# The seam between the expert loop and the second block: residual by identity products, both norms of a tile from one pass

## The chip, the cores and the metric

One core of one Trainium2 chip runs the whole program. The metric is the device time of one execution in microseconds; the kernel before took 2886.91 us (median of three, 2886.65 to 2887.95). The engines are TensorE (PE, and PEld for its weight loads), VectorE (DVE), ScalarE (ACT), GpSimd (POOL) and SyncE (SP), which issues most DMAs. PSUM has eight banks of 128x512 f32, called `bank[0]` to `bank[7]`.

## The reference

Two blocks run one after the other on a sequence of 512 tokens of width 1024. The first ends with an expert layer and a norm; the second starts, in each of its two layers, with a norm of the same `x`:

```
x = x + gt2 * expert_choice_ffn(h, w_router, w_gate, w_up, w_down)
x = rms_norm(x, g_final)                     # end of the first block
h = rmsnorm(x, mix_norm_g[0])                # start of the second block
x = x + mixing_layer(h, ...)                 # x itself is needed again here
```

`rms_norm(x, g)` is `x * rsqrt(mean(x*x) + 1e-6) * g`. The expert layer has 16 experts with 64 tokens each; each expert's result is scaled by its gate and added to the rows of the tokens it took.

## The kernel before

Tokens lie in four tiles of 128 (`TT = 4`); `x` stays on chip as [128, 4, 1024]. Experts run in pairs (`PAIRS = 8`), two experts side by side on 64 rows each. Per pair PE multiplies `xeT` by eight chunks of 1 MB of `w_gate` and eight of `w_up`, turns `hid`, and multiplies `hidT` by eight chunks of `w_down` (`chunk_pair`, line 1804, two chunks at a time). Chunks arrive by DMA in a ring of eight. DVE gates the result into `ye` (L2569), ACT rounds it to `ye_hi` (L721, `split_ye`), DVE takes the rest, `ye_lo` (L2573), and PE scatters both to token rows with `scat_now` in eight pieces of 128x512, `piece = 2 * tile + half` (`scatter`, L1774 and L1775). DVE adds each piece to `x` (`add_scattered`, L2544). For pairs 0 to 6 this is hidden behind the next pair's products; for the last pair it stands alone.

Each engine has its own instruction list, written out by hand and run in order; semaphores (`wait_ge`, `then_inc`) join them. The seam after the last pair goes tile by tile. ACT sums the squares of `x` and takes the root (`tile_rms`, L1004 and L1006), DVE inverts and scales `x` by it and by `g_final` (`moe_scaled`, L2599 and L2601), ACT sums squares of the scaled `x` (`tile_sum`), DVE makes a diagonal matrix of the second norm's factors (`make_diag`, L2577 and L2579), PE turns and scales the tile by it (`turn_tile`, L1889), DVE applies the gain (`take_tile`, L2589, into `h_tmp`), ACT rounds it to `hT_hi` (`tile_hi`) and DVE takes the rest, `hT_lo` (`tile_lo`, L2595). Then PE starts the projections of layer 0 (L1544, L1548, L1549: three products of rounded operands per block). `first_projection` covers the first two tiles, 48 products of 256 columns; it stands behind the turning of all four tiles. What follows waits for all of `hT_lo`.

The weights of the second block come as chunks of 1 MB into `raw[0..3]`. ACT rounds chunk m to `w_hi[m % 2]` (`split(m)`, L721) and POOL takes the rest, `w_lo` (L709). The loads of the first chunks start when PE has used up all but four of the last `w_down` chunks (the POOL engine's wait for `N_LAYER - RING + RAW`); `w_hi[0]` and `w_lo[0]` lie in ring slots of chunks 4 and 5 of the last `w_down`.

## Time and profile before

| | us |
|---|---|
| median of three runs | 2886.91 |
| lowest and highest run | 2886.65, 2887.95 |
| profiled execution | 2892.95 |
| its span | 2891.0 |
| PE busy | 2699.0 (93%) |
| DVE, ACT, POOL busy | 1096.4, 829.0, 697.6 |
| last product of the expert loop starts to run its last chunk | 1631.08 |
| PE goes on without waiting for `hT_lo` | 1671.10 |

The profile is of one execution. Times in the rows are us from the start of the span. A timeline row gives start, duration, engine, line, operation, written and read tiles, how many instructions the row merges, and in brackets how long the engine had been idle and who released it. Busy times of PE are modelled ends of pipelined matmuls, so the distance between starts says more than a duration. PEclk is the granted clock of TensorE: 1.00 is 2.4 GHz and 0.5 is 1.2 GHz.

### The profile page before, as it was taken

To read this page: it belongs to the slowest core of one execution; us is meant where nothing else is said; L and a number is where in the kernel's file an instruction comes from. 1 tells how busy PE (TensorE), PEld (TensorE's weight loads), DVE (VectorE), ACT (ScalarE), POOL (GpSimd) and SP (SyncE) were. 2 spreads that over 40 slices of the span, in tenths; PEclk is the share of its full clock that TensorE was granted. 3 is DMA by queue.
4 is the path that set the end of the run, shared out by engine and by line. 5 is a ranking of instruction groups with operands and counts; after the bars stand their busy time and mean duration, and the time that the engine had idled before them with its cause. 6 is when DMAs were issued, how large, how long until landed. Compare 5 with 4: busy or idle time off the path is not lost.

```text
span 2891.0 us, 35167 instructions
## 1 busy us (share of the span) xinstructions
PE 2699.0 (93%) x14496; PEld 2014.6 (70%) x14496; DVE 1096.4 (38%) x1800; ACT 829.0 (29%) x1444; POOL 697.6 (24%) x297
## 2 busy tenths in 40 slices
PE   7999999999989996999999799999999998999998
PEld 4777777786447885444444397888878896988877
DVE  3555555533341124112121488420014697300034
ACT  2433333333333222000000224532222327322122
POOL 2222222220013410000000032233434332343433
PEclk8999999999999997999999999999999999999999
DMA  7111111102012323899999721123222221223221
GB/s 256 52 58 58 58 58 58 36 30 80 27 39 78 127 92 131 351 409 409 409 408 409 293 84 63 59 73 102 88 96 94 73 88 44 74 89 101 89 100 44
DMA packets 212563, 382.38 MB, mean 132 GB/s; under 512 B 10833, under 2 KB 145877, under 8 KB 211413
## 3 DMA queue, kind: packets, MB, share of 16 engines
q1 hardware_dynamic: 211088, 379.06, 36.4%
q8 instruction: 95, 1.56, 0.2%
q10 hardware_dynamic: 1349, 1.51, 0.2%
q14 instruction: 31, 0.25, 0.0%
HBM read 378.44 MB, written 2.10 MB: 132 GB/s over the span
## 4 chain that ended last, share of the span: by engine, by line
PE 69%; DMA 8%; issue 7%; DVE 5%; PEld 5%; ACT 3%; POOL 2%; DVEq 1%; PEldq 0%; SPq 0%; ACTq 0%; POOLq 0%
PE bank L1544 14%; PE bank L1548 13%; PE bank L1549 13%; PE bank L1804 7%; DMA ring<-in_w_up 4%; DMA ring<-in_w_gate 3%; PE bank L1749 2%; PE bank L1692 2%; PEld bank L1352 2%; PE bank L1412 1%; PE bank L1421 1%; PE bank L1598 1%; PE bank L1425 1%; PE bank L1615 1%; PE bank L1318 1%
## 5 line engine op out<-in xcount | busy, mean ns | idle before, releaser
L709 POOL TENSOR_TENSOR w_lo<-ring,w_hi 128x2048 fp32r<-128x2048 f32 x96 | 446.3, 4649 | 1279.0 <-ACT w_hi L721 1279.0
L721 ACT ACTIVATE w_hi<-ring 128x2048 fp32r<-128x2048 f32 (+1 forms) x114 | 215.0, 1886 | 676.4 <-PE bank L1544 676.3
L1544 PE MATMUL bank<-hT_hi,w_hi 128*128 128x512 f32 (+1 forms) x928 | 357.1, 385 | 9.2 <-DVE hT_lo L2595 7.7
L1548 PE MATMUL bank<-hT_lo,w_hi 128*128 128x512 f32 (+1 forms) x928 | 352.8, 380 | 0.0
L1549 PE MATMUL bank<-hT_hi,w_lo 128*128 128x512 f32 (+1 forms) x928 | 349.4, 377 | 0.0
L1804 PE MATMUL bank<-ring,xeT 128*64 128x512 f32 x992 | 225.5, 596 | 30.8 <-DMA ring<-in_w_gate 18.5
L1544 PEld LDWEIGHTS bank<-hT_hi,w_hi 128*128 128x128 f32 x928 | 175.8, 189 | 45.7 <-DVE hT_lo L2595 8.5
L2786 DVE TENSOR_TENSOR ffn_hT<-ffn_sg,bank 128x512 f32<-128x512 f32 x44 | 30.3, 688 | 449.1 <-PE bank L1549 449.1
L1549 PEld LDWEIGHTS bank<-hT_hi,w_lo 128*128 128x128 f32 x928 | 175.5, 189 | 35.7
L1548 PEld LDWEIGHTS bank<-hT_lo,w_hi 128*128 128x128 f32 x928 | 174.9, 189 | 31.8 <-issue 1.0
L1804 PEld LDWEIGHTS bank<-ring,xeT 128*64 128x64 f32 x992 | 77.0, 137 | 155.5 <-issue 152.9
L1318 PE MATMUL bank<-hT,head_w 128*128 128x512 f32 x336 | 157.0, 593 | 0.0
L678 POOL TENSOR_TENSOR w_lo<-ring,w_hi 128x2048 fp32r<-128x2048 f32 x16 | 73.6, 4602 | 331.5 <-ACT w_hi L721 331.5
L2780 DVE TENSOR_TENSOR ffn_lo<-ffn_hT,ffn_hi 128x1024 fp32r<-128x1024 f32 x22 | 98.1, 4457 | 118.6 <-ACT ffn_hi L721 118.6
L1544 PE MATMUL bank<-w_hi,ffn_hi 128*128 128x512 f32 x352 | 138.1, 392 | 4.0 <-DVE ffn_lo L2780 4.0
L1548 PE MATMUL bank<-w_lo,ffn_hi 128*128 128x512 f32 x352 | 137.7, 391 | 0.0
L1549 PE MATMUL bank<-w_hi,ffn_lo 128*128 128x512 f32 x352 | 137.6, 391 | 0.0
L1804 PE MATMUL bank<-ring,hidT 128*64 128x512 f32 x512 | 112.3, 594 | 3.8 <-DMA ring<-in_w_down 2.9
L1544 PE MATMUL bank<-w_hi,hT_hi 128*128 128x256 f32 x384 | 109.2, 284 | 5.0 <-POOL w_lo L709 3.3
L2645 DVE SCALAR_TENSOR_TENSOR conf<-glu,cols_l,conf 128x512 f32<-128x512 f32 x120 | 111.3, 957 | 6.6 <-issue 1.3
L655 POOL TENSOR_TENSOR intra<-decay,tri 128x512 f32<-128x512 f32 x16 | 20.3, 1266 | 384.5 <-ACT decay L844 384.5
L1549 PE MATMUL bank<-w_hi,hT_lo 128*128 128x256 f32 x384 | 108.3, 282 | 0.0
(492 smaller groups left out, 5058.2 us busy)
## 6 DMA issues: line engine op xcount, KB each, us to landing
ring<-in_w_gate SPq DMA_DIRECT2D x86, 1024.0 KB, 9.1
ring<-in_w_down SPq DMA_DIRECT2D x86, 1024.0 KB, 14.1
ring<-in_w_up SPq DMA_DIRECT2D x82, 1024.0 KB, 14.1
ring<-in_w_in SPq DMA_DIRECT2D x33, 1024.0 KB, 5.2
head_w<-in_w_in SPq DMA_DIRECT2D x32, 512.0 KB, 5.3
mod_w<-in_w_mod SPq DMA_DIRECT2D x8, 2048.0 KB, 8.5
ring<-in_w_out SPq DMA_DIRECT2D x12, 1024.0 KB, 4.8
ring<-in_w_mod SPq DMA_DIRECT2D x8, 1024.0 KB, 16.4
```

Of the source, the lines that this page charges most:

```text
L678: pool.tensor_tensor(w_lo[m % 2][:], raw[merge_raw(m)[0]][:], w_hi[m % 2][:].bitcast(F32), ALU.subtract).then_inc(lo_ready, 1)
L709: pool.tensor_tensor(w_lo[m % 2][:], raw[m % RAW][:], w_hi[m % 2][:].bitcast(F32), ALU.subtract).then_inc(lo_ready, 1)
L721: return act.activation(dst, src, ACT.Copy)
L1318: last = mm(bank[0 if s == 1 else 1][:], head_w[:, k, s * HD:(s + 1) * HD], hT[:, k, :], start=k == 0, stop=k == KD - 1)
L1352: last = mm(bank[2][:, t * P:(t + 1) * P], hT[:, k, t * P:(t + 1) * P], head_w[:, k, 3 * HD:4 * HD], start=k == 0, stop=k == KD - 1)
L1544: first = mm(dst, a[0], b[0], start=start, stop=False)
L1548: mm(dst, a[0], b[1], start=False, stop=False)
L1549: return mm(dst, a[1], b[0], start=False, stop=stop)
L1692: last = mm(bank[t % 2 * 2 + c // 2][:, c % 2 * 256:(c % 2 + 1) * 256], mT[:, k, t * P:(t + 1) * P], kview(N_OUT + c)[:, k, :], start=k == ...
L1804: last = mm(bank[banks + hf][a * 64:a * 64 + 64, :], lhs[:, 2 * j + kk, a * 64:a * 64 + 64], chunk[a][:, kk, hf * 512:(hf + 1) * 512], sta ...
L2645: stt(conf[:, b, :], glu[:, b, j:j + SEQ], w, conf[:, b, :], ALU.mult, ALU.add)
L2780: tt(ffn_lo[:, j % 2], ffn_hT[:, 2 * j:2 * j + 2, :], ffn_hi[:, j % 2].bitcast(F32), ALU.subtract)\
```

## The change

PE: after the last pair's transposes, `keep` copies `x` into banks by products with the identity (four products of 128x512 before the down projection, two after its first chunk pair, two after its end), and the last pair's scatter accumulates on them, piece n in bank n. `scatter` no longer waits for DVE's adds. `turn_tile` uses banks 2t and 2t+1 for the first norm.

DVE: in place of adding a piece to `x`, `moe_gained` multiplies the bank by `g_final` into `x`. `moe_eps` makes the term that takes the place of epsilon, from the sum of squares of the unscaled tile. The norm's factor itself (`rstd[:, 4:8]`) is computed once for the four tiles at the end.

ACT: a table load for the root stands behind the last pair's last copy, `split(0)` stands ahead of `split_ye` (it waits for the sixth of the eight last `w_down` chunks to be used up), `moe_sums` sums the squares of both banks of a tile and of the gained tile, and takes one root. The copies `ident_r` and `causal_r` move behind the last tile. `x` is multiplied by the factors of the first norm in four activations between the second sigmoid and `split(3)` of layer 0.

The diff:

```diff
--- before.py
+++ after.py
@@ -1059,17 +1059,17 @@
                 copy(hidT[:, 0:4, :].rearrange("p k n -> p (k n)"), bank[0][:]).then_inc(sem("hidT_act"), 1)
                 if pair + 1 < PAIRS:
                     gathered(pair + 1)
-            split_ye(PAIRS - 1)
-
-
-            reached(act, "block2_consts")
-            copy(ident_r[:], ident[:])
-            copy(causal_r[:], causal[:]).then_inc(step["mask_parts"], 1)
+            LAST = (PAIRS - 1) * 8
+            act.activation(rms[:, 0:1], eps_col[:, 0:1], ACT.Sqrt)
 
             def split(m):
 
                 act.wait_ge(raw_landed[m % RAW], 16 * (6, 6, 2, 2)[m % RAW] + 16 * (l * PER_LAYER // RAW + m // RAW + 1))
-                parts_free(act, m, l)
+                if l + m == 0:
+
+                    act.wait_ge(chunk_used, N_LAYER - 2)
+                else:
+                    parts_free(act, m, l)
                 copy(w_hi[m % 2][:], raw[m % RAW][:]).then_inc(hi_ready, 1)
 
             def tile_sum(n, t):
@@ -1095,21 +1095,39 @@
                 parts_free(act, M_DOWN + j, l)
                 copy(ffn_hi[:, j % 2], ffn_hT[:, 2 * j:2 * j + 2, :]).then_inc(sem("ffn_hi_ready"), 1)
 
+            def moe_sums(t):
+
+                act.wait_ge(sem("scattered"), LAST + 2 * t + 2)
+                act.drain()
+                for hf in (1, 0):
+                    if hf == 0:
+                        act.wait_ge(sem("x_added"), LAST + 2 * t + 1)
+                    act.activation(sq_junk[:, hf * 512:(hf + 1) * 512], bank[2 * t + hf][:], ACT.Square,
+                                   accum_out=ss[:, 4 * hf + t:4 * hf + t + 1]).then_inc(sem("moe_rms"), 1)
+                act.wait_ge(sem("x_added"), LAST + 2 * t + 2)
+                act.drain()
+                act.activation(sq_junk[:], x[:, t, :], ACT.Square, accum_out=ss[:, 8 + t:9 + t])
+                act.wait_ge(sem("x_tile"), TT + t + 1)
+                act.drain()
+                act.activation(rms[:, t:t + 1], ss[:, 8 + t:9 + t], ACT.Sqrt, scale=1.0 / DM, bias=pinv2[:, t, 1:2])\
+                    .then_inc(sem("rms_ready"), 1)
+
             l = 0
             split(0)
-            act.activation(sq_junk[:, 0:1], eps_col[:, 0:1], ACT.Sqrt)
-            for t in range(TT):
-                act.wait_ge(sem("x_added"), (PAIRS - 1) * 8 + 2 * t + 2)
-                act.drain()
-                tile_rms(4 + t, t, "moe_rms")
-                if t:
-                    tile_sum(0, t - 1)
-                if t >= 2:
-                    tile_hi(0, t - 2)
-            tile_sum(0, TT - 1)
-            tile_hi(0, TT - 2)
+            split_ye(PAIRS - 1)
+            moe_sums(0)
+            moe_sums(1)
+            tile_hi(0, 0)
+            moe_sums(2)
+            tile_hi(0, 1)
+            moe_sums(3)
+            tile_hi(0, 2)
             split(1)
-            tile_hi(0, TT - 1)
+            tile_hi(0, 3)
+            act.activation(rms[:, 4:8], pinv2[:, 0:TT, 0], ACT.Sqrt, scale=1.0 / DM).then_inc(sem("moe_rms"), 1)
+            reached(act, "block2_consts")
+            copy(ident_r[:], ident[:])
+            copy(causal_r[:], causal[:]).then_inc(step["mask_parts"], 1)
             for l in range(LAYERS):
                 cols_l, lam_i = cols_ls[l], lam_is[l]
                 for b in range(2):
@@ -1118,6 +1136,11 @@
                         .then_inc(sem("glu_sig"), 1)
                     if b == 0:
                         split(2)
+                if l == 0:
+                    act.wait_ge(sem("x_added"), PAIRS * 8 + 1)
+                    act.wait_ge(sem("turned"), 3 * KD)
+                    for t in range(TT):
+                        act.activation(x[:, t, :], x[:, t, :], ACT.Copy, scale=rstd[:, 4 + t:5 + t])
                 for m in range(3, 7):
                     split(m)
 
@@ -1763,7 +1786,15 @@
                     last = mm(bank[4][:, 0:EXPERTS], onehot[:, t, pair * P:(pair + 1) * P], aff[:, t, :], start=t == 0, stop=t == TT - 1)
                 last.then_inc(sem("slots_done"), 1)
 
-            def scatter(pair, piece, dst):
+            def keep(pieces):
+
+                for piece in pieces:
+                    t, hf = piece // 2, piece % 2
+                    if piece >= 6:
+                        pe.wait_ge(sem("ye_gated"), 2 * PAIRS - 2 + hf + 1)
+                    mm(bank[piece][:], ident[:], x[:, t, hf * 512:(hf + 1) * 512], start=True, stop=False)
+
+            def scatter(pair, piece, dst, start=True):
 
                 t, hf = piece // 2, piece % 2
                 if piece == 0:
@@ -1771,7 +1802,7 @@
                 if piece < 2:
                     pe.wait_ge(sem("ye_ready"), pair * 2 + hf + 1)
                 rows, cols = scat_now[:, t * P:(t + 1) * P], slice(hf * 512, (hf + 1) * 512)
-                mm(dst, rows, ye_hi[:, cols], start=True, stop=False)
+                mm(dst, rows, ye_hi[:, cols], start=start, stop=False)
                 mm(dst, rows, ye_lo[:, cols], start=False, stop=True).then_inc(sem("scattered"), 1)
 
             def scatter_behind(pair, pieces):
@@ -1829,16 +1860,20 @@
                         last.then_inc(sem("hid_turned"), 1)
                 if pair + 1 < PAIRS:
                     gather(pair + 1, 1)
+                else:
+                    pe.wait_ge(sem("scat_ready"), PAIRS)
+                    keep((2, 3, 4, 5))
                 pe.wait_ge(sem("hidT_act"), pair + 1)
                 pe.wait_ge(sem("hidT_dve"), pair + 1)
                 for j in range(4):
                     chunk_pair(2, hidT, 6, j)
+                    if pair + 1 == PAIRS and j == 0:
+                        keep((0, 1))
             pe.drain()
             pe.sem_inc(parts_used, 2)
+            keep((6, 7))
             for piece in range(8):
-                if piece >= 4:
-                    pe.wait_ge(sem("x_added"), (PAIRS - 1) * 8 + piece - 3)
-                scatter(PAIRS - 1, piece, bank[piece % 4][:])
+                scatter(PAIRS - 1, piece, bank[piece][:], start=False)
 
 
             reached(pe, "block2_consts")
@@ -1882,8 +1917,8 @@
             def turn_tile(n, t, free_parts=False):
 
                 pe.wait_ge(sem("diag_ready"), n * TT + t + 1)
-                b0 = 2 * t if n and n % 2 == 0 else 2 * (t % 2) + (0 if n else 4)
-                if t >= 2 and (n % 2 or not n):
+                b0 = 2 * (t % 2) if n % 2 else 2 * t
+                if t >= 2 and n % 2:
                     pe.wait_ge(sem("h_ready"), n * KD + 2 * (t - 2) + 2)
                 for k in range(KD):
                     last = mm(bank[b0 + k // 4][:, k % 4 * P:(k % 4 + 1) * P], x[:, t, k * P:(k + 1) * P], diag[:, t, :],
@@ -2581,7 +2616,7 @@
             def take_tile(n, t):
 
                 dve.drain()
-                b0 = 2 * t if n and n % 2 == 0 else 2 * (t % 2) + (0 if n else 4)
+                b0 = 2 * (t % 2) if n % 2 else 2 * t
                 gains = cols_ls[n // 2][:, L_FFN if n % 2 else L_MIX:]
                 for hf in range(2):
                     dve.wait_ge(sem("turned"), (n + 2) * KD + 2 * t + hf + 1)
@@ -2594,32 +2629,44 @@
                     ks, ts_ = slice(4 * hf, 4 * hf + 4), slice(t * P, (t + 1) * P)
                     tt(hT_lo[:, ks, ts_], h_tmp[:, hf], hT_hi[:, ks, ts_].bitcast(F32), ALU.subtract).then_inc(sem("hT_lo_ready"), 1)
 
-            def moe_scaled(t):
-                dve.wait_ge(sem("moe_rms"), t + 1)
-                dve.reciprocal(rstd[:, 4 + t:5 + t], rms[:, 4 + t:5 + t])
-                dve.drain()
-                stt(x[:, t, :], x[:, t, :], rstd[:, 4 + t:5 + t], gfin_b[:], ALU.mult, ALU.mult)
-                dve.drain().then_inc(sem("x_tile"), 1)
+            def moe_gained(t):
+                for hf in range(2):
+                    c = slice(hf * 512, hf * 512 + 512)
+                    dve.wait_ge(sem("scattered"), (PAIRS - 1) * 8 + 2 * t + hf + 1)
+                    if hf:
+                        dve.wait_ge(sem("moe_rms"), 2 * t + 1)
+                    tt(x[:, t, c], bank[2 * t + hf][:], gfin_b[:, c], ALU.mult).then_inc(sem("x_added"), 1)
+
+            def moe_eps(t):
+
+                dve.wait_ge(sem("moe_rms"), 2 * t + 2)
+                ts(pinv2[:, t, 0:1], ss[:, t:t + 1], ss[:, 4 + t:5 + t], DM * EPS, ALU.add, ALU.add)
+                dve.drain()
+                ts(pinv2[:, t, 1:2], pinv2[:, t, 0:1], EPS / DM, None, ALU.mult).then_inc(sem("x_tile"), 1)
 
             dve.wait_ge(sem("row_b_in"), 64)
-            for t in range(TT):
-                for piece in (2 * t, 2 * t + 1):
-                    add_scattered(PAIRS - 1, piece, bank[piece % 4][:])
-                if t:
-                    moe_scaled(t - 1)
-                if t >= 2:
-                    make_diag(0, t - 2)
-                if t == 3:
-                    take_tile(0, 0)
-                    tile_lo(0, 0)
-            moe_scaled(3)
+            moe_gained(0)
+            moe_eps(0)
+            moe_gained(1)
+            make_diag(0, 0)
+            moe_eps(1)
+            take_tile(0, 0)
+            make_diag(0, 1)
+            moe_gained(2)
+            tile_lo(0, 0)
+            moe_eps(2)
+            take_tile(0, 1)
             make_diag(0, 2)
-            take_tile(0, 1)
+            moe_gained(3)
             tile_lo(0, 1)
+            moe_eps(3)
+            take_tile(0, 2)
             make_diag(0, 3)
-            for t in (2, 3):
-                take_tile(0, t)
-                tile_lo(0, t)
+            tile_lo(0, 2)
+            take_tile(0, 3)
+            tile_lo(0, 3)
+            dve.wait_ge(sem("moe_rms"), 2 * TT + 1)
+            dve.reciprocal(rstd[:, 4:8], rms[:, 4:8]).then_inc(sem("x_added"), 1)
             reached(dve, "block2_consts")
             dve.drain()
             rope_buf = rope_2
```

On ACT, from the last `hidT` copy of the expert loop to the roots of the first two tiles. Before (`sq_junk,ss<-x` is the sum of squares of a tile, `rms` its root, `w_hi_210<-ring_52` is `split(0)`):

```order
L721 ACTIVATE hidT<-bank 128x512
L721 ACTIVATE ye_hi<-ye 128x512 x2
L721 ACTIVATE ident_r<-ident 128x128
L721 ACTIVATE causal_r<-causal 128x128
L721 ACTIVATE w_hi_210<-ring_52 128x2048
L1100 ACT_TABLE_LOAD
L1100 ACTIVATE sq_junk<-eps_col 128x1
L1004 ACTIVATE sq_junk,ss<-x 128x1024
L1006 ACTIVATE rms<-ss,eps_col 128x1
L1004 ACTIVATE sq_junk,ss<-x 128x1024
L1006 ACTIVATE rms<-ss,eps_col 128x1
L1004 ACTIVATE sq_junk,ss<-x 128x1024
```

After:

```order
L721 ACTIVATE hidT<-bank 128x512
L1063 ACT_TABLE_LOAD
L1063 ACTIVATE rms<-eps_col 128x1
L721 ACTIVATE w_hi_210<-ring_52 128x2048
L721 ACTIVATE ye_hi<-ye 128x512 x2
L1105 ACTIVATE sq_junk,ss<-bank 128x512 x2
L1109 ACTIVATE sq_junk,ss<-x 128x1024
L1112 ACTIVATE rms<-ss,pinv_227 128x1
L1105 ACTIVATE sq_junk,ss<-bank 128x512 x2
L1109 ACTIVATE sq_junk,ss<-x 128x1024
L1112 ACTIVATE rms<-ss,pinv_227 128x1
```

`split(0)` and the table load now stand ahead of the two `ye_hi`, and one root per tile stands where two stood, behind two sums from banks and one from `x`.

On DVE, from the last `ye` to the first rounded rest. Before (`x<-x,bank` adds two pieces of a tile, `x<-x,rstd,gfin_b` scales it):

```order
L2569 SCALAR_TENSOR_TENSOR ye<-bank,gate_col,gt_b 128x512 x2
L2573 TENSOR_TENSOR ye_lo<-ye,ye_hi 128x512 x2
L2544 TENSOR_TENSOR x<-x,bank 128x512 x4
L2599 RECIPROCAL rstd<-rms 128x1
L2601 SCALAR_TENSOR_TENSOR x<-x,rstd,gfin_b 128x1024
L2544 TENSOR_TENSOR x<-x,bank 128x512 x2
L2599 RECIPROCAL rstd<-rms 128x1
L2601 SCALAR_TENSOR_TENSOR x<-x,rstd,gfin_b 128x1024
L2577 RECIPROCAL rstd<-rms 128x1
L2579 TENSOR_SCALAR diag<-ident,rstd 128x128
```

After (`x<-bank,gfin_b` is the gained tile, `pinv_227` holds the epsilon term):

```order
L2604 SCALAR_TENSOR_TENSOR ye<-bank,gate_col,gt_b 128x512 x2
L2608 TENSOR_TENSOR ye_lo<-ye,ye_hi 128x512 x2
L2638 TENSOR_TENSOR x<-bank,gfin_b 128x512 x2
L2643 TENSOR_SCALAR pinv_227<-ss 128x1
L2645 TENSOR_SCALAR pinv_227<-pinv_227 128x1
L2638 TENSOR_TENSOR x<-bank,gfin_b 128x512 x2
L2612 RECIPROCAL rstd<-rms 128x1
L2614 TENSOR_SCALAR diag<-ident,rstd 128x128
L2643 TENSOR_SCALAR pinv_227<-ss 128x1
L2645 TENSOR_SCALAR pinv_227<-pinv_227 128x1
L2624 TENSOR_TENSOR h_tmp<-bank,cols_l 128x512 x2
L2612 RECIPROCAL rstd<-rms 128x1
```

The scaling by the first norm and its reciprocal are gone from between the tiles, and the first `h_tmp` stands before the third tile's pieces.

## Rows read from the trace of the kernel before

**Rows 1.** The page's busy times: engine, us, share of span, instructions.

```profile
PE 2699.0 (93%) x14496; PEld 2014.6 (70%) x14496; DVE 1096.4 (38%) x1800; ACT 829.0 (29%) x1444; POOL 697.6 (24%) x297
```

**Rows 2.** Stages: length; busy PE, PEld, DVE, ACT, POOL; PEclk, DMA share, GB/s.

```profile
1641.15:1648.40 7.25, 0.00 (x0) 0.02 (x1) 5.75 (x9) 5.73 (x13) 2.55 (x1) 0.66 0.48 157
1648.40:1654.80 6.40, 6.35 (x32) 6.17 (x32) 5.45 (x10) 3.25 (x7) 0.00 (x0) 0.58 0.47 150
1654.80:1663.20 8.40, 5.30 (x31) 5.12 (x32) 6.56 (x13) 5.20 (x12) 0.00 (x0) 0.80 0.01 2
```

**Rows 3.** Timeline of PE, last pair's transposes to first scatter.

```profile
1615.06 1.25 PE L1827 MATMUL bank<-ident,hid 128*128 128x128 f32 x8 [0.79 <-DVE hid L2561]
1617.14 7.38 PE L1804 MATMUL bank<-ring,hidT 128*64 128x512 f32 x32 [0.83 <-ACT hidT L721]
1625.96 3.65 PE L1804 MATMUL bank<-ring,hidT 128*64 128x512 f32 x16 [1.45 <-DMA ring<-in_w_down]
1631.08 3.65 PE L1804 MATMUL bank<-ring,hidT 128*64 128x512 f32 x16 [1.47 <-DMA ring<-in_w_down]
1637.07 0.47 PE L1774 MATMUL bank<-ye_hi,scat_now 128*128 128x512 f32 x1 [2.33 <-DVE ye_lo L2573]
```

**Rows 4.** Timeline of DVE in the seam.

```profile
1637.87 2.48 DVE L2544 TENSOR_TENSOR x<-x,bank 128x512 f32<-128x512 f32 x4 [0.29 <-PE bank L1775]
...
1642.43 2.35 DVE L2601 SCALAR_TENSOR_TENSOR x<-x,rstd,gfin_b 128x1024 f32<-128x1024 f32 x1
...
1646.33 1.28 DVE L2601 SCALAR_TENSOR_TENSOR x<-x,rstd,gfin_b 128x1024 f32<-128x1024 f32 x1
...
1658.85 1.29 DVE L2595 TENSOR_TENSOR hT_lo<-h_tmp,hT_hi 128x512 fp32r<-128x512 f32 x2
```

**Rows 5.** Timeline of ACT in the seam.

```profile
1637.16 1.90 ACT L721 ACTIVATE w_hi<-ring 128x2048 fp32r<-128x2048 f32 x1
...
1640.64 1.06 ACT L1004 ACTIVATE sq_junk<-x 128x1024 f32<-128x1024 f32 x1
...
1641.86 0.30 ACT L1006 ACTIVATE rms<-ss,eps_col 128x1 f32<-128x1 f32 x1
...
1662.19 1.23 ACT L721 ACTIVATE hT_hi<-h_tmp 128x512 fp32r<-128x512 f32 x2 [1.38 <-DVE h_tmp L2589]
```

**Rows 6.** Timelines of POOL, DVE and PE: weight rests, last `hT_lo`, its waiter.

```profile
1639.14 4.56 POOL L709 TENSOR_TENSOR w_lo<-ring,w_hi 128x2048 fp32r<-128x2048 f32 x1 [517.77 <-ACT w_hi L721]
...
1665.31 4.58 POOL L709 TENSOR_TENSOR w_lo<-ring,w_hi 128x2048 fp32r<-128x2048 f32 x1 [21.61 <-ACT w_hi L721]
...
1665.78 4.66 DVE L2595 TENSOR_TENSOR hT_lo<-h_tmp,hT_hi 128x512 fp32r<-128x512 f32 x1 [0.25 <-ACT hT_hi L721]
...
1671.10 0.38 PE L1544 MATMUL bank<-hT_hi,w_hi 128*128 128x256 f32 x1 [1.95 <-DVE hT_lo L2595]
```

**Rows 7.** Timelines elsewhere: f32 products, a turned tile, a 512-wide activation with accumulator.

```profile
517.30 4.03 PE L1318 MATMUL bank<-hT,head_w 128*128 128x512 f32 x9
...
1661.43 2.05 PE L1889 MATMUL bank<-diag,x 128*128 128x128 f32 x16 [0.47 <-DVE diag L2579]
...
1776.06 0.72 ACT L1144 ACTIVATE p<-bank,nmax 128x512 f32<-128x512 f32 x1
```

**Rows 8.** Line 573 from 1620 to 1660: the first five raw loads.

```profile
L573 SPq DMA_DIRECT2D ring<-in_w_in x5: 367/583/3912, 1624.6 to 1644.1; - x5
...
DMA to landing us min/median/max: 5.3/9.4/12.7
```

**Rows 9.** ACT in layer 0: timeline; last row by line (busy us, mean ns).

```profile
1688.15 0.69 ACT L1117 ACTIVATE sig<-bank,cols_l 128x512 f32<-128x512 f32 x1 [3.34 <-PE bank L1549]
1690.23 1.92 ACT L721 ACTIVATE w_hi<-ring 128x2048 fp32r<-128x2048 f32 x1 [1.39 <-PE bank L1544]
1701.65 1.92 ACT L721 ACTIVATE w_hi<-ring 128x2048 fp32r<-128x2048 f32 x1 [9.51 <-PE bank L1544]
...
L727 ACT ACTIVATE xn<-x 128x1024 f32<-128x1024 f32 x4 | 4.2, 1041 | 0.0
```

## The prediction

> **What bounds the kernel now.** Read first the busy shares: TensorE (PE) is busy 93% of the span [rows 1], so only a stretch where PE idles can give time back without removing PE work. The change touches one such stretch, the seam between the expert loop and layer 0 of the second block. The stages [rows 2] show it: PE is busy 0 of 7.25 us, then 6.35 of 6.40 (at a mean granted clock of 0.58, so mostly at 1.2 GHz), then 5.30 of 8.40. Before the seam PE waits for DMA: in the last down projection it stands idle 1.45 and 1.47 us for `in_w_down`, and 0.83 us for `hidT` [rows 3]. After it PE works without holes from 1671.10, when it stops waiting for the last `hT_lo` [rows 6]. So the time that counts runs from 1634.73, the end of the last expert product (1631.08 + 3.65, [rows 3]), to 1671.10: **36.4 us**. I judge the change by when this second point comes. Up to the last pair's down projection both kernels issue the same work.
>
> In between four engines hand one tile on to the next. VectorE (DVE) makes `ye` and `ye_lo`, PE scatters, DVE adds, ScalarE (ACT) sums squares for the first norm, DVE scales `x`, ACT sums for the second norm, DVE makes `diag`, PE turns the tile, DVE and ACT split it. Then `split(1)` on ACT (1.90 us as `split(0)`, [rows 5]) wakes GpSimd (POOL), and the last `hT_lo` is caught behind POOL's 4.58 us [rows 6].
>
> **Part 1, the identity products.** `keep` puts `x` into the eight banks by eight products of 128x512 in f32. The nearest row is the f32 product of the same shape, 9 records in 4.03 us [rows 7], or 0.45 us each. An f32 product is two records: one turned tile is 8 products in the program and 16 records in 2.05 us [rows 7]. So one identity product costs 0.90 us and six of them, placed before the end of the down projection, cost 5.4. Idle time to hide in is 0.83 + 1.45 + 1.47 = 3.75 [rows 3]. Step by step: the transposes are through at 1616.2, `keep(2..5)` runs to 1619.8, chunks 0 and 1 of w_down (3.65 each) surround `keep(0,1)` and end at 1628.9 in place of 1624.5, chunk 2 ends at 1632.5 and chunk 3 at **1636.2, not 1634.73: +1.5 us**. Bounds: 0 if a product is one record (2.7 us for six, all hidden), 1.7 if all of 5.4 − 3.75 shows. I take 1.5.
>
> The Trainium skill ("FP8 and Floating Point Precision", TensorE Precision Notes) says that true FP32 takes four passes, and "TensorE: Matmul & The Clock Gate" (Wait — 56ns, not 53.3ns?) gives 215.7 ns for 512 columns; by these one product is 0.86 us (an estimate) and this part costs 0.2 us less.
>
> **Part 2, the first weight split moved ahead of `split_ye`.** `split(0)` needs `raw[0]`. Its load is issued when chunk 1 of w_down is used up, at 1624.60 before, and landed 9.4 us later, at 1634.0, because it queues behind w_down; an undisturbed one takes 5.3 [rows 8]. Now it is issued at 1629.0 and lands at about 1634.3. ACT then splits for 1.90 us [rows 5], to 1636.25, and is free when `ye_gated` comes at 1637.0, so ACT itself delays nobody. But POOL starts `w_lo` 0.08 us after a split ends and holds on for 4.56 us [rows 6]: 1636.3 to 1640.9. The next thing that DVE must do is `ye_lo` from `ye` and `ye_hi`, ready at 1637.7. What happens to a DVE operation with two SBUF inputs under POOL's `w_lo` is in the rows: the `x` scaling took 2.35 us where the others took 1.28 [rows 4] and ended 1.08 after POOL; `hT_lo` took 4.66 where two take 1.29 [rows 4, 6] and ended 0.55 after POOL. Adds from a bank, with one SBUF input, kept their pace, four in 2.48 us, although POOL was on for half of that [rows 4, 6]. So `ye_lo` waits until 1640.9 + 0.55 = 1641.45, and the first scatter starts at **1641.5 in place of 1637.07 [rows 3]: +4.4 us**. This swallows the 1.5 us of part 1, since `raw[0]`, not PE, sets the time. Bounds: 1.8 without the hold (PE finishes `keep(6,7)` at 1638.8), 4.9 if `raw[0]` lands 0.5 later. I take 4.4. The Trainium skill ("SBUF — State Buffer", Who interferes with whom) says that whichever of the two starts first keeps the shared ports for its whole instruction. The rule speaks against this place for the split, and the rows bear it out.
>
> The other side: the same `w_lo` no longer holds up the first `x` scaling (1.07 us), and `split(0)` and the load of a function table behind it no longer stand between `ye_hi` and the first norm on ACT, which started at 1640.64 though its tile was complete by 1639.2 (1637.87 and two adds, [rows 4, 5]). Both gains lie inside the next part.
>
> **Part 3, both norms at once.** Removed per tile: one reciprocal and the 1.28 us scaling on DVE, and the round trip ACT, DVE, ACT between the two norms. Added: two Squares of 512 from banks on ACT, the two small `pinv2` operations on DVE. Prices: a 512-wide activation from a bank with accumulator took 0.72 [rows 7] (I use 0.76 for the one behind a drain and 0.68 for the next); Square of 1024 with its read 1.22 (from start to start, [rows 5]) and the root 0.33; DVE 0.65 for a bank operation (2.48 / 4, [rows 4]) and 0.42 for the `pinv2` pair (two small ones of about 0.2, priced like a reciprocal); a turned tile 1.95 at 2.4 GHz. I wrote out both orders engine by engine, each instruction starting 0.04 us after the later of its engine and its releaser. For the kernel before, with its own slow clock stretches, this gives 1671.1 against 1671.10, so the bookkeeping holds.
>
> For the kernel after, from the first scatter at 1641.5: two pieces 1.2, tile 0's sums and root 3.2, tile 1's 3.1 (1649.0), waiting for tile 0 turned and split 2.2, tile 2 5.2, tile 3 5.2, so `hT_hi` of tile 2 is done at 1661.6. Before, that point was 1663.42 (1662.19 + 1.23, [rows 5]), or 26.35 us after the first scatter; now 20.1. **−6.3 us.** Behind it nothing is new: split 1.9, POOL 4.6, `hT_lo` 1.3, which gives 1669.4. The 48 products of the first projection (5.6 us) start at 1663.5 and end at 1669.1, just as late: no more can be won here without both.
>
> Sum: +4.4 − 6.3 + 0.2 (rounding over the tail) = **−1.7 us** at full clock.
>
> **Part 4, what moves behind the seam.** ACT scales `x` in four activations of 1.04 [rows 9], 4.2 us between the second sigmoid and `split(3)`. That split started at 1690.23, the next one waited for PE until 1701.65 [rows 9]. 4.2 us after the sigmoid's end at 1688.8 means start 1693.0, then 1.9 + 4.9 on POOL: ready at 1699.9, needed at 1701.6. Hidden, with 1.7 us left; if that cover goes, it costs what exceeds it. DVE's long convolution loses its POOL overlap a little differently; I add 0.2. And the clock: with the scatter at +4.4 PE idles some 2.7 us, and tiles are turned in short bursts 5 us apart, so a slow stretch over one burst is likely. The mean of 0.80 over 8.40 us before the first projection [rows 2] means 3.4 us at 1.2 GHz; laid over one tile after another such a piece costs the chain 0 to 1.4; I add 0.5. **Net −1.0 us.**
>
> **Rivals.** (A) **No hold**: DVE gets through, or `w_lo` comes too late to meet `ye_lo`. Against it stand the two held operations of rows 4 and 6, for it only a DVE that is ready before POOL is. The scatter starts at 1638.8, the chain is then bound by the first projection and ends at 1666.5: −4.6, 2882.3; with cheap products as well −6.2, 2880.7. (B) **The clock stays at 1.2 GHz** from the hold through the turned tiles and into the first projection. For it: in the stretch before, it stayed low through tile turning that kept PE busy 6.35 of 6.40 us [rows 2]. Through the turns only, it costs 3.5 and gives +1.8, 2888.7. If it stays low through the 48 products too, they take 11.2 us: +9.0, 2895.9. It decides from the moment PE enters the first projection, at 0.5 us lost per us: to be slower by 5.8 us takes 8 of those 11 us at 1.2 GHz. (C) **The cost falls on layer 0**: `split(3)` slips past its 1.7 us and PE waits: −1.0 + 1 to 4, 2887 to 2890. (D) The removed round trip wins less, since Squares from banks take 1.1 us, not 0.7: +2.0, 2887.9.
>
> **How the numbers follow.** The profiled execution took 2892.95 (span 2891.0 and 1.95 around it), 6.0 above the median of 2886.91; a shift of 1 us is carried over to the median as it is. Forecast 2886.91 − 1.0 = **2885.9**. A measurement of this kernel can tell 0.2%, 5.8 us, from no change. Chances: forecast within 2 us 0.52; A 0.16, of which 0.04 beyond −5.8; B 0.12, of which 0.06 beyond +5.8; C and D 0.11; something that I don't see 0.09, of which 0.06 faster and 0.02 slower. So faster 0.10, same 0.82, slower 0.08. The range reaches to A and to the mild end of B and C: 2881.8 to 2890.5.
>
> **What would show it.** Right: `keep` records of about 0.45 us pitch and the last expert product ending 1.5 us later; POOL's `w_lo` starting before `ye_lo`, and `ye_lo` at 3.5 to 4.5 us; the first scatter 4.4 later; the tail from first scatter to `hT_hi` of tile 2 at 20 us; no new PE wait for `w_lo` behind `split(3)`. Wrong: `ye_lo` at 0.7 us, a PE wait for POOL near 1700, or a granted clock of 0.5 inside the first projection.

## The result, and the profile after

| | before | after |
|---|---|---|
| median of 15 runs each, us | 2888.74 | 2892.73 |
| lowest and highest, us | 2885.19, 2893.35 | 2889.35, 2898.01 |
| profiled execution, its span, us | 2892.95, 2891.0 | 2892.73, 2890.9 |
| PE, DVE, ACT, POOL busy, us | 2699.0, 1096.4, 829.0, 697.6 | 2703.8, 1099.2, 833.2, 697.1 |

The changed kernel is **slower by 4 us**: the ratio is 1.0014, interval [1.0007, 1.002]. The forecast was 1 us faster, 2885.9, worked out from a median of three runs (2886.91); fifteen runs of the kernel before give 2888.74. The result is less than the 5.8 us that the prediction took as the least that can be told, but its interval lies wholly above 1. Forecast and result are both small against the runs' own scatter of 8 us, and the two profiled executions differ by 0.1 us in span. That the spans agree is chance: from 2278.41 to 2299.50, far behind the change, the trace of before has a stretch at a mean granted clock of 0.66 (2285 to 2290), and the same distance between two `w_lo` is 21.09 us there and 19.58 after. So the place is read from distances inside each trace, not from the spans.

The page's busy times of the kernel after [answers rows 1] show PE up by 4.8 us (the identity products are 7.6, and less of the seam ran at the slow clock: the mean granted clock from 1640 to 1680 is 0.91 instead of 0.83) and ACT up by 4.2, about the scaling of `x` (the norms' own work on ACT is 12.3 us before and 12.6 after):

```profile
PE 2703.8 (94%) x14512; PEld 2012.7 (70%) x14512; DVE 1099.2 (38%) x1801; ACT 833.2 (29%) x1453; POOL 697.1 (24%) x297
```

**The seam on PE**, timeline of after [rows 3]: start, duration, operation, number merged, idle time before and its releaser.

```profile
1614.59 1.25 PE L1858 MATMUL bank<-ident,hid 128*128 128x128 f32 x8 [0.79 <-DVE hid L2596]
1615.68 3.60 PE L1795 MATMUL bank<-x,ident 128*128 128x512 f32 x8
...
1624.71 10.52 PE L1835 MATMUL bank<-ring,hidT 128*64 128x512 f32 x48
1636.11 1.98 PE L1795 MATMUL bank<-x,ident 128*128 128x512 f32 x4 [0.88 <-DVE ye L2604]
1641.18 0.47 PE L1805 MATMUL bank<-ye_hi,scat_now 128*128 128x512 f32 x1 [3.09 <-DVE ye_lo L2608]
...
1656.13 3.60 PE L1924 MATMUL bank<-diag,x 128*128 128x128 f32 x16 [3.11 <-DVE diag L2614]
...
1669.15 0.39 PE L1567 MATMUL bank<-hT_hi,w_hi 128*128 128x256 f32 x1
```

The waits for `in_w_down` of rows 3 are gone: the products of the last three chunk pairs run in one piece, which ends at 1635.23. The row at 1669.15 is where PE goes on with the tiles that need all of `hT_lo`; before, that was 1671.10. I measure the seam from the transposes of the last pair to this row, since what happens ahead of it differs only by chance: 56.04 us before (1671.10 − 1615.06), **54.56 after: 1.48 us won**.

**Who held whom**, timelines of DVE, ACT and POOL in the same stretch of after:

```profile
1636.75 4.89 DVE L2608 TENSOR_TENSOR ye_lo<-ye,ye_hi 128x512 fp32r<-128x512 f32 x2
...
1663.99 5.11 DVE L2630 TENSOR_TENSOR hT_lo<-h_tmp,hT_hi 128x512 fp32r<-128x512 f32 x2
```

```profile
1633.99 1.91 ACT L721 ACTIVATE w_hi<-ring 128x2048 fp32r<-128x2048 f32 x1 [16.60 <-DMA ring<-in_w_in]
...
1660.24 1.23 ACT L721 ACTIVATE hT_hi<-h_tmp 128x512 fp32r<-128x512 f32 x2 [0.44 <-DVE h_tmp L2624]
1661.37 1.90 ACT L721 ACTIVATE w_hi<-ring 128x2048 fp32r<-128x2048 f32 x1
```

```profile
1635.98 4.51 POOL L709 TENSOR_TENSOR w_lo<-ring,w_hi 128x2048 fp32r<-128x2048 f32 x1 [515.39 <-ACT w_hi L721]
```

`w_lo` starts before `ye_lo`, and `ye_lo` ends at 1641.64 in place of about 1638.1 (as in experiment 2). From the first scatter (1641.18) to the end of `hT_hi` of tile 2 (1661.47) the new order of the norms takes 20.3 us. Two stages of this stretch, scatter and first projection [rows 2], with the granted clock third from the end:

```profile
1641.20:1645.50 4.30, 4.30 (x13) 3.33 (x14) 2.69 (x6) 2.62 (x7) 0.00 (x0) 0.67 0.89 287
...
1660.00:1669.20 9.20, 7.76 (x65) 7.56 (x65) 8.86 (x11) 6.06 (x9) 4.59 (x1) 1.00 0.02 3
```

**Layer 0** gives it back and more. Here are DVE and POOL before, in the stretch with the long convolution (`conf`, 18 operations between the second `glu` and the first `rope`), and then after:

```profile
1692.58 0.75 DVE L2633 SCALAR_TENSOR_TENSOR glu<-bank,cols_l,sig 128x512 f32<-128x512 f32 x1
1693.42 4.00 DVE L2643 TENSOR_SCALAR conf<-glu,cols_l 128x512 f32<-128x512 f32 x1
1697.49 18.17 DVE L2645 SCALAR_TENSOR_TENSOR conf<-glu,cols_l,conf 128x512 f32<-128x512 f32 x18
...
1716.93 3.48 DVE L2662 TENSOR_TENSOR rot<-rope 128x256 f32<-128x256 f32 x1
...
1726.72 4.69 DVE L2662 TENSOR_TENSOR rot<-rope 128x256 f32<-128x256 f32 x1
...
1731.91 1.41 DVE L2645 SCALAR_TENSOR_TENSOR conf<-glu,cols_l,conf 128x512 f32<-128x512 f32 x2 [0.17 <-issue]
```

```profile
1692.22 4.90 POOL L709 TENSOR_TENSOR w_lo<-ring,w_hi 128x2048 fp32r<-128x2048 f32 x1 [2.59 <-ACT w_hi L721]
1703.65 4.83 POOL L709 TENSOR_TENSOR w_lo<-ring,w_hi 128x2048 fp32r<-128x2048 f32 x1 [6.53 <-ACT w_hi L721]
1715.08 5.05 POOL L709 TENSOR_TENSOR w_lo<-ring,w_hi 128x2048 fp32r<-128x2048 f32 x1 [6.60 <-ACT w_hi L721]
```

After:

```profile
1690.67 0.74 DVE L2680 SCALAR_TENSOR_TENSOR glu<-bank,cols_l,sig 128x512 f32<-128x512 f32 x1
1691.51 0.55 DVE L2690 TENSOR_SCALAR conf<-glu,cols_l 128x512 f32<-128x512 f32 x1
1692.14 26.86 DVE L2692 SCALAR_TENSOR_TENSOR conf<-glu,cols_l,conf 128x512 f32<-128x512 f32 x18
...
1724.76 4.73 DVE L2709 TENSOR_TENSOR rot<-rope 128x256 f32<-128x256 f32 x1
...
1732.24 5.88 DVE L2692 SCALAR_TENSOR_TENSOR conf<-glu,cols_l,conf 128x512 f32<-128x512 f32 x8 [0.17 <-issue]
```

```profile
1692.94 4.61 POOL L709 TENSOR_TENSOR w_lo<-ring,w_hi 128x2048 fp32r<-128x2048 f32 x1 [5.22 <-ACT w_hi L721]
1701.74 4.96 POOL L709 TENSOR_TENSOR w_lo<-ring,w_hi 128x2048 fp32r<-128x2048 f32 x1 [4.19 <-ACT w_hi L721]
1713.17 4.62 POOL L709 TENSOR_TENSOR w_lo<-ring,w_hi 128x2048 fp32r<-128x2048 f32 x1 [6.47 <-ACT w_hi L721]
```

Read the two against each other. ACT's scaling of `x` (4.26 us) pushes `split(3)` back by 2.7 us against the sigmoid ahead of it (part of the 4.26 falls in time in which ACT had waited for PE), so `w_lo` starts 2.27 us after `glu` instead of 0.36 us before it. Then all three `w_lo` lie wholly over the convolution. Before, the first one lay partly over `glu` and the third partly over the first `rope` operations, and those read a bank and keep their pace (0.75, 0.68) while POOL is on. What DVE lost to POOL from `glu` to the next piece of the convolution was 16.0 us before: 3.45 (4.00 − 0.55), 5.2 (18.17 less 18 at about 0.72), 3.05 and 4.26 (the two `rot`, 0.43 each when free). It is 18.2 after: 13.9 and 4.30. From `glu` to that next piece DVE takes **41.57 us instead of 39.33**.

PE is waiting for that chain. Waits of PE over layer 0 of the kernel after (total, times, longest):

```profile
PE bank L2014 <- DVE p L2729: 3.1, 3, 1.5
PE bank L1977 <- DVEq L2711: 2.2, 1, 2.2
```

The second row is new (PE turns the rotated keys, which DVE finishes last). The first stood at 2.2, twice, before; more on it below.

That all of DVE's delay reaches PE could have been read before the change. Here are the last `rot` of DVE and PE's turning of the keys before, then PE after:

```profile
1749.43 0.42 DVE L2663 TENSOR_TENSOR rot<-rope 128x256 f32<-128x256 f32 x1
1749.93 1.97 PE L1942 MATMUL bank<-ident,rot 128*128 128x128 f32 x16
```

```profile
1750.27 1.97 PE L1977 MATMUL bank<-ident,rot 128*128 128x128 f32 x16 [2.16 <-DVEq L2711]
```

Before, DVE was through at 1749.85 and PE began at 1749.93, straight behind its previous product: there was no slack between them worth naming.

To compare kernels I use two distances: the **seam** as above, and **layer 0** from there to the start of the `w_lo` that POOL begins near 1790 (released through ACT by PE's progress).

| kernel | seam | layer 0 | sum against before |
|---|---|---|---|
| before | 56.04 | 121.02 | 0 |
| after | 54.56 | 124.44 | +1.94 |

So 1.48 us won and 3.42 lost, in one execution each. The medians say +4.0 ± 2.

### The profile page after: what moved, and what is told of

Its sections match the earlier page's. It is cut to its first block, busy times and chain, and to the rows that moved or that the text cites. A ratio compares the mean times of both kernels' runs of the same rounds, so it can differ in the third digit from the quotient of the medians.

```text
span 2890.9 us, 35208 instructions
## 1 busy us (share of the span) xinstructions
PE 2703.8 (94%) x14512; PEld 2012.7 (70%) x14512; DVE 1099.2 (38%) x1801; ACT 833.2 (29%) x1453; POOL 697.1 (24%) x297
## 4 chain that ended last, share of the span: by engine, by line
PE 66%; DMA 8%; DVE 8%; issue 7%; PEld 5%; ACT 3%; DVEq 2%; POOL 2%; PEldq 0%; SPq 0%; ACTq 0%; POOLq 0%
PE bank L1567 13%; PE bank L1571 12%; PE bank L1572 12%; PE bank L1835 7%; DMA ring<-in_w_up 4%; DMA ring<-in_w_gate 3%; PE bank L1772 2%; PE bank L1715 2%; PEld bank L1375 2%; DVE conf L2692 2%; PE bank L1435 1%; PE bank L1444 1%; PE bank L1621 1%; PE bank L1448 1%; PE bank L1638 1%
## 5 line engine op out<-in xcount | busy, mean ns | idle before, releaser
L2692 DVE SCALAR_TENSOR_TENSOR conf<-glu,cols_l,conf 128x512 f32<-128x512 f32 x120 | 124.7, 1069 | 6.2 <-issue 0.7
L655 POOL TENSOR_TENSOR intra<-decay,tri 128x512 f32<-128x512 f32 x16 | 20.3, 1266 | 383.7 <-ACT decay L844 383.7
```

The costliest lines, as they stand in the source:

```text
L2692: stt(conf[:, b, :], glu[:, b, j:j + SEQ], w, conf[:, b, :], ALU.mult, ALU.add)
```

## The experiments

All were timed in five rounds beside the kernel before; its median was 2890.28 in those of experiments 1 to 4 and 2889.0 in those of 5 to 7. Seam and layer 0 stand in one table behind the texts.

**1. The scaling of `x` later.** After, with the four activations behind `split(6)`:

```diff
+                for m in range(3, 7):
+                    split(m)
                 if l == 0:
                     act.wait_ge(sem("x_added"), PAIRS * 8 + 1)
                     act.wait_ge(sem("turned"), 3 * KD)
                     for t in range(TT):
                         act.activation(x[:, t, :], x[:, t, :], ACT.Copy, scale=rstd[:, 4 + t:5 + t])
-                for m in range(3, 7):
-                    split(m)
```

> The changed kernel with one thing moved: the four activations that scale x on ACT stand behind split(6) of layer 0 instead of ahead of split(3). Theory (layer 0): in the profile of the changed kernel the seam wins 1.5 us, but VectorE's convolution and rotation, which stand under GpSimd's weight rests, end 2.2 us later against PE, because split(3) is 2.7 us later and its weight rest, with the two behind it, lies wholly over operations with two SBUF inputs. Then here the second PE wait for rot (2.2 us) is gone or under 0.5 us, and the time is 2 to 3.4 us below the changed kernel, so about 2.0 us (0.07%) above to 0.5 us below the kernel before. Rival (the phases of GpSimd and VectorE fall that way whatever ACT does): the wait for rot stays near 2 us and the time stays at ratio 1.0014 to the kernel before.

Measured: 2890.19 against 2890.28, ratio 1.0 [0.9991, 1.0009]. The convolution is back in its old place under POOL, and PE has no wait for `rot`. Layer 0 is 2.26 us shorter than in the kernel after. Timeline of DVE of this kernel:

```profile
1688.91 4.00 DVE L2690 TENSOR_SCALAR conf<-glu,cols_l 128x512 f32<-128x512 f32 x1
1692.98 18.18 DVE L2692 SCALAR_TENSOR_TENSOR conf<-glu,cols_l,conf 128x512 f32<-128x512 f32 x18
```

**2. The first split behind `split_ye`.** After, with `split(0)` one line lower:

```diff
-            split(0)
             split_ye(PAIRS - 1)
+            split(0)
             moe_sums(0)
```

> The changed kernel with split(0) behind split_ye, as in the kernel before. Theory (the hold): ye_lo is not held, takes 1.35 us for two instead of 4.9; the first scatter comes about 2.5 us earlier than in the changed kernel (bound by keep(6,7)); GpSimd's first weight rest runs from about 1639.3 to 1643.9 and may hold the small pinv2 operations by up to 2 us. The last hT_lo comes 1 to 2.6 us earlier. In time: 0 to 2.6 us below the changed kernel. Rival (layer 0 is the bound whatever the seam does): the seam shortens, PE waits longer for rot, and the time does not move.

Measured: 2886.57, ratio 0.999 [0.9981, 0.9999]. `ye_lo` is free, `w_lo` follows it:

```profile
1636.79 1.35 DVE L2608 TENSOR_TENSOR ye_lo<-ye,ye_hi 128x512 fp32r<-128x512 f32 x2
```

```profile
1639.30 4.58 POOL L709 TENSOR_TENSOR w_lo<-ring,w_hi 128x2048 fp32r<-128x2048 f32 x1 [518.30 <-ACT w_hi L721]
```

The seam shrinks to 51.32, 3.24 less than after and more than the 1 to 2.6 expected: the first scatter comes 22.99 us behind the transposes instead of 26.59, so 3.6 earlier and not 2.5, and the small `pinv2` operations were not held. Layer 0 stays at the bad value, 124.40, with the same wait for `rot`.

**3. Both edits.**

> Both edits on the changed kernel: split(0) behind split_ye, x scaled behind split(6). If the hold on ye_lo and the displaced split(3) are the two costs, they add: 3 to 6 us below the changed kernel, that is 0 to 3 us below the kernel before (ratio 0.999 to 1.000). If layer 0's VectorE chain swallows what the seam wins whatever order ACT takes: ratio 1.0005 to 1.0015.

Measured: 2884.98, ratio **0.9986 [0.9977, 0.9995]**. The two gains add: seam 51.32, layer 0 122.19. This is faster than both kernels, and by more than the 0 to 3 us expected against before (5.3 by the medians, 3.55 by the two distances).

**4. The scaling alone, in the kernel before.** Four copies of `x` onto itself (nothing is scaled; they change no value) between the second sigmoid and `split(3)`:

```diff
                     if b == 0:
                         split(2)
+                if l == 0:
+                    for t in range(TT):
+                        act.activation(x[:, t, :], x[:, t, :], ACT.Copy)
                 for m in range(3, 7):
```

> The kernel before, with four activations added on ACT (x copied onto itself) between the second sigmoid and split(3) of layer 0, where the changed kernel scales x. Nothing else is touched, so this prices the displaced split(3) alone. Theory (layer 0): VectorE's convolution and rotation end about 2 us later, PE waits 1 to 3 us for rot, ratio 1.0004 to 1.0012. Rival (hidden, as forecast: 1.7 us of slack for the weight rest, PE not waiting for GpSimd): ratio 1.0000 within 0.0003.

Measured: 2892.86, ratio 1.001 [1.0001, 1.0019]. The seam is that of before (56.06), layer 0 is 124.96. The four copies take 3.89 us and `split(3)` starts 2.3 us later behind the sigmoid than before. DVE, the turning of the keys on PE, and PE's new wait in layer 0 of this kernel:

```profile
1689.95 26.76 DVE L2648 SCALAR_TENSOR_TENSOR conf<-glu,cols_l,conf 128x512 f32<-128x512 f32 x18
```

```profile
1748.08 3.32 PE L1945 MATMUL bank<-ident,rot 128*128 128x128 f32 x16 [2.16 <-DVEq L2667]
```

```profile
PE bank L1945 <- DVEq L2667: 2.2, 1, 2.2
```

So the wait for `rot` needs nothing of the seam: **moving ACT's split alone makes PE wait 2.16 us**, as in the kernel after. The rest of the 3.94 us that layer 0 loses here is not the same as there. Right behind the wait PE turned the keys at the slow clock (a mean granted clock of 0.52 from 1750 to 1752), in 3.32 us instead of 1.97, so 1.35 us come from that. In the traces of after and of experiment 2 the same wait was followed by full clock.

**5. The hold alone, in the kernel before.** `split(0)` ahead of `split_ye`, with its wait as in the changed kernel; norms and residual as before:

```diff
-            split_ye(PAIRS - 1)
...
             l = 0
             split(0)
+            split_ye(PAIRS - 1)
```

> The kernel before with one edit: split(0) on ACT stands ahead of split_ye, as in the changed kernel; norms, residual and the rest as before. Theory (GpSimd's hold alone costs the seam what it was forecast at): w_lo starts near 1636, ye_lo takes 4 to 5 us instead of 1.4, the first scatter starts 3.5 to 4.5 us later; the first x scaling is then no longer held (1.3 us instead of 2.35) and the tail is shorter by 0.5 to 1.5, so the point where PE stops waiting for hT_lo comes 2 to 4 us later, and layer 0 stays as it was: 2.5 to 3.5 us slower than before (a ratio of 1.001). Rival (the seam absorbs the hold, because the norms' chain has slack against split(1) and its w_lo): that point moves by under 1 us and the time is that of before.

Measured: 2892.74 against 2889.0, ratio 1.0011 [1.0002, 1.0019]. DVE, then PE:

```profile
1633.55 5.18 DVE L2574 TENSOR_TENSOR ye_lo<-ye,ye_hi 128x512 fp32r<-128x512 f32 x2 [0.23 <-ACT ye_hi L721]
```

```profile
1638.27 0.77 PE L1775 MATMUL bank<-ye_hi,scat_now 128*128 128x512 f32 x1 [6.41 <-DVE ye_lo L2574]
```

The first scatter comes 26.13 us behind the transposes (1612.14) against 22.01 before: +4.12. The tail from there to `hT_hi` of tile 2 is 1.77 shorter, and the seam is 58.38, +2.34. So the place of `split(0)` is worth 2.3 us in the old order and 3.2 in the new one, in one execution each.

**6. All eight identity products behind the loop**, on top of experiment 3:

```diff
-                    keep((2, 3, 4, 5))
...
-                    if pair + 1 == PAIRS and j == 0:
-                        keep((0, 1))
...
-            keep((6, 7))
+            keep((0, 1, 2, 3, 4, 5, 6, 7))
```

> The version with both edits (split(0) behind split_ye, x scaled behind split(6)), and in addition all eight identity products stand behind the last down projection, none in it. Theory (the six early ones are nearly hidden by DMA waits): without them the last expert product ends 0.5 to 1.5 us earlier than with them, but eight exposed products of 0.90 us push the first scatter from about 1 us behind ye_lo to 7.2 us behind the end of the loop, 3.5 to 4.5 us later than with them early; the total is 3 to 4 us above the version with both edits, 2888 to 2889. Rival (the chain behind the scatter has that much slack): under 1 us.

Measured: 2890.09 against 2889.0, ratio 1.0002 [0.9993, 1.001]. Timeline of PE of this kernel:

```profile
1614.24 1.26 PE L1858 MATMUL bank<-ident,hid 128*128 128x128 f32 x8 [0.79 <-DVE hid L2593]
...
1630.34 3.65 PE L1835 MATMUL bank<-ring,hidT 128*64 128x512 f32 x16 [1.51 <-DMA ring<-in_w_down]
1634.11 7.13 PE L1795 MATMUL bank<-x,ident 128*128 128x512 f32 x16
```

The loop's last product ends 19.75 us behind the transposes (19.67 before); with six products inside it is 20.64 (after). So six products cost **0.9 us** where they stand, in idle time that DMA leaves, and putting them behind the loop costs 3.4 us more (seam 54.68 against 51.32). The waits for `in_w_down` are back.

**7. One tap fewer ahead of a `w_lo`**, on top of experiment 3. Layer 0 still lost 1.2 us there. The piece of the convolution between the second and third attention tile takes 7.20 us in the kernel after, 2.90 before:

```profile
1770.80 7.20 DVE L2692 SCALAR_TENSOR_TENSOR conf<-glu,cols_l,conf 128x512 f32<-128x512 f32 x4
```

```profile
1772.84 4.62 POOL L709 TENSOR_TENSOR w_lo<-ring,w_hi 128x2048 fp32r<-128x2048 f32 x1 [12.84 <-ACT w_hi L721]
```

and before:

```profile
1770.22 2.90 DVE L2645 SCALAR_TENSOR_TENSOR conf<-glu,cols_l,conf 128x512 f32<-128x512 f32 x4
```

```profile
1772.48 5.06 POOL L709 TENSOR_TENSOR w_lo<-ring,w_hi 128x2048 fp32r<-128x2048 f32 x1 [12.82 <-ACT w_hi L721]
```

Before, the fourth operation started some 0.1 us ahead of `w_lo`; after, the piece started 0.22 us later relative to it and missed. The reverse shows as well: `w_lo` before, which began while the fourth operation was on, took 5.06 us instead of 4.62. The edit:

```diff
-                        long_conv(24 + 2 * n, min(26 + 2 * n, CONF_K))
+                        long_conv((24, 26, 27, 29)[n], (26, 27, 29, CONF_K)[n])
```

> The version with both edits (split(0) behind split_ye, x scaled behind split(6)), and in addition DVE's last seven taps of the 31-tap convolution in both layers are cut as 2, 1, 2, 2 between the first four attention tiles, instead of 2, 2, 2, 1. Theory (the 1.1 us that layer 0 still gives back is a near miss: the convolution piece of four operations that took 7.20 us instead of 2.90 because its last operation started just after w_lo did): the piece, now two operations, is through before w_lo starts, PE's wait for p near 1770 goes, layer 0 gives nothing back, and the total is about 1 us below the version with both edits, 2884. Rival (that DVE is the bound over these tiles anyway, whatever is held): the wait moves to the next tile and the total stays within 0.3 us.

Measured: **2883.96** against 2889.0, ratio **0.998 [0.9971, 0.9989]**. PE's wait for `p` is at 2.2 again, twice, and layer 0 at 121.05, the value of before:

```profile
PE bank L2014 <- DVE p L2729: 2.2, 2, 1.5
```

The 1.0 us below experiment 3 (another batch) can't be told apart by the medians alone; the trace shows it. In this trace the clock took part back elsewhere: the stages from 1800 to 1820 and from 1820 to 1840 had a mean granted clock of 0.95 and 0.88 where before had 1.00, and two `w_lo` around them lie 27.22 us apart (1819.98 and 1847.20) where before had 24.49.

| kernel | seam | layer 0 | sum against before | median against before |
|---|---|---|---|---|
| after | 54.56 | 124.44 | +1.94 | +4.0 |
| 1 scaling later | 54.91 | 122.18 | +0.03 | −0.1 |
| 2 split(0) behind | 51.32 | 124.40 | −1.34 | −3.7 |
| 3 both | 51.32 | 122.19 | −3.55 | −5.3 |
| 4 before, scaling added | 56.06 | 124.96 | +3.96 | +2.6 |
| 5 before, split(0) ahead | 58.38 | 121.08 | +2.40 | +3.7 |
| 6 both, products late | 54.68 | 122.16 | −0.22 | +1.1 |
| 7 both, one tap moved | 51.75 | 121.05 | −4.26 | −5.0 |

The first sum is of one execution each, the second of 11 to 15 runs with an uncertainty of some 2 to 3 us. They agree within 2.5 us and make the same kernels faster (2, 3, 7) and slower (after, 4, 5). So the two distances hold what the edits do, up to that uncertainty and to slow pieces of the clock inside them, like the 1.35 us of experiment 4.

## Why the prediction was right in the seam and wrong in all

- **Part 1, the identity products.** Priced right (8 records in 3.60 us, 0.45 each, 0.90 a product); the loop's end came 0.97 later (20.64 against 19.67), not 1.5, because chunks that follow each other without a gap are 3.51 us apart (10.52 / 3) and I had counted 3.65 for each of four. Experiment 6 shows the same 0.9. Behind the hold little of it was left, but not nothing: without the products (experiment 5) `w_lo` starts 20.94 us behind the transposes, with them (after) 21.39, and the first scatter 26.13 and 26.59.
- **Part 2, the hold.** Right: `w_lo` at 1635.98 (forecast 1636.3), the first half of `ye_lo`, for which the scatter waits, through 0.55 behind POOL's end (1641.04 and 1640.49), the first scatter +4.58 against the transposes (forecast +4.4). The length of `ye_lo`, 4.89, is above the 3.5 to 4.5 named, mostly because it started 0.95 us earlier. Experiments 2 and 5 show the cause: `ye_lo` takes 1.35 us when `w_lo` comes behind it and 5.18 when `w_lo` comes first. The rule that I cited there says that the side that starts first keeps the shared ports for its whole instruction (the Trainium skill, "SBUF — State Buffer", Who interferes with whom). These figures agree with it; which operations of DVE are held is taken up in the last section. Rival A, no hold, falls. The price without the hold was put at 1.8, and it was 1.0 (experiment 2: 22.99 against 22.01).
- **Part 3, both norms at once.** 20.3 us from the first scatter to `hT_hi` of tile 2, forecast 20.1; it was 26.35 before. With `split(0)` in its old place (experiment 2) the new order takes 20.6, so 5.7 of the 6.1 us come with the new order itself. Squares from banks took 0.59 to 0.60 each, not 1.1: the Squares of rival D fall.
- **The clock.** The slow pieces came (PEclk 0.67 over the scatter, one turned tile in 3.60 instead of 2.05). What they cost the chain no run separates; the first projection ran at full clock (1.00 from 1660.00 to 1669.20). Rival B falls. Its larger figure doesn't follow from its parts: +1.8 and 5.6 us for 48 products at half the clock are +7.4, not +9.0. Seam: −1.7 forecast, −1.2 with the clock's 0.5, −1.48 measured.
- **Part 4 is the step that failed.** I wrote that DVE's long convolution loses its POOL overlap a little differently and added 0.2. It measured 2.24 on DVE, of which PE waited 2.16, and 1.2 more further on, 3.4 in all. I had asked whether `split(3)` keeps its own deadline and it did: the wait of PE for `w_lo` did not grow (3.2 us in two waits, before and after), and rival C in its wording (the split slips, PE waits for it) did not occur. What moved was where POOL's 4.6 us falls on DVE. Rival C had the place and the size, 1 to 4 us, but the wrong carrier. I gave the term 0.2 without a row, though the rows of DVE in that stretch stood in the trace, and without asking who waits for DVE there: PE turned the keys 0.08 us after DVE had finished them. It also isn't so that PE works without holes behind the seam, as I wrote: before, it idles 1.66 us for `w_lo` at 1689.78 and 0.84 at 1738.32. Experiment 4 isolates the 2.16 in a kernel whose seam is untouched, and experiment 1 takes 2.26 back by moving nothing but the scaling.

With the measured 3.4 for that term the sum would have been −1.7 + 0.5 + 3.4 = +2.2, and the median at 2889.1 within 2 us of the 2890.9 that the ratio gives. What is left to the medians' +4.0 lies within their interval (1.0007 is +2.0).

One point stays open. Of the last 1.2 us of layer 0, experiment 7 shows that the late operation under `w_lo` carries it. The 0.22 us by which DVE reached that piece later are pauses marked "issue": in the kernel after one of 0.44 us ahead of `p` at 1765.50 and none ahead of the next `conf`, in the kernel before none and 0.22 (1765.36). All kernels made from after have the first pattern and experiments 4 and 5, made from before, the second. Why it differs no run shows.

## What to carry to other kernels

When an operation is added to the engine that releases another (here ACT ahead of POOL), it isn't enough that the released work still meets its own deadline: look at what lies under its new position on the engine that it holds up, and at who waits for that. Put such long operations over ones that read PSUM, and keep them off the last two-input SBUF operation that a chain needs. In the seam it took one line (`split(0)` behind `split_ye`) to get 3.2 us more, and in layer 0 one moved block and another cut of the taps to get 3.4 back.

## What the runs showed of the hardware

- **What POOL's `w_lo` holds up is finer than "DVE".** In the trace of experiment 7 the two `pinv` operations of one element per partition and the product from a bank run at full pace though `w_lo` is on from 1637.40 to 1641.97 (the two narrow ones read one SBUF tensor each):

```profile
1638.19 0.69 DVE L2638 TENSOR_TENSOR x<-bank,gfin_b 128x512 f32<-128x512 f32 x1 [0.70 <-ACT sq_junk L1105]
1638.80 0.20 DVE L2643 TENSOR_SCALAR pinv<-ss 128x1 f32<-128x1 f32 x1
1639.08 0.15 DVE L2645 TENSOR_SCALAR pinv<-pinv 128x1 f32<-128x1 f32 x1
```

  while in that of experiment 3 an operation just as narrow, but a SCALAR_TENSOR_TENSOR of three SBUF operands, ends 0.02 us behind the `w_lo` that runs from 1782.24 to 1786.79:

```profile
1783.56 3.25 DVE L2727 SCALAR_TENSOR_TENSOR mix<-psum,lam_i,pinv 128x1 f32<-128x1 f32 x1
```

- **A wide operation with one SBUF input is held too**: TENSOR_SCALAR `conf<-glu`, 128x512, took 4.00 us under `w_lo` and 0.55 without. So width or the number of inputs alone doesn't tell which are held; the runs don't separate them further.
- **A shift of 0.2 us can decide over 4.3 us on DVE.** The piece that experiment 7 cuts took 2.90 or 7.20 us by whether its last operation started ahead of `w_lo`; on PE it was worth 1.1. A shift upstream can tip it either way, so a forecast of under a few us should name such near misses downstream.
- **A wait of the same length was followed by either clock.** PE idled 2.16 us ahead of the turning of the keys in after, experiment 2 and experiment 4; the 16 products then took 1.97 us in the first two and 3.32 in the third.
